# Routing by tile beside w_out, expert 0's rows from one-hot products, and the first norm interleaved with the first chunks

## The chip, the cores and the metric

The kernel runs on one core of a Trainium2 chip. The metric is the device time of one execution in microseconds (us). One execution was also recorded by the hardware profiler; its rows are what is quoted below. PE is TensorE, DVE VectorE, ACT ScalarE, POOL GpSimd, SP SyncE.

## The reference, cut to what matters

Input x is 512 tokens by 1024 features, all in float32.

```python
h = layer_norm(x, ln_in_g, ln_in_b)
proj = h @ w_in            # 1024 x 9240: q, k, v, gates of two mixers
y_gla = gla_branch(...) @ w_gla_proj      # gated linear attention, 4 heads, chunks of 64
y_fox = fox_branch(...) @ w_fox_proj      # causal attention with forgetting, 8 heads
mixed = sigmoid(z_gla) * y_gla + sigmoid(z_fox) * y_fox
h = layer_norm(ALPHA * h + mixed @ w_out, ln_mix_g, ln_mix_b)
logits = h @ w_router + b_router          # 32 experts
top_val, top_idx = top_k(logits, 4); gates = softmax(top_val)
# every token goes to its 4 experts: ((clip(up) + 1) * glu(gate)) @ w_down[e] + b_down[e]
h = layer_norm(ALPHA * h + sum_of_gated_experts, ln_ffn_g, ln_ffn_b)
```

## The kernel before

Each engine has its own hand-written instruction list; semaphores tie them together, and the lists set the order. The 512 tokens are four tiles (TT = 4) of 128 partitions.

**Products.** A product with weights is done in three passes (`passes`, L1282 to L1284): each operand is split into a high part (ACT copies it to float32r, `whi`, `hT_hi`, `xT_hi`) and a low part (DVE subtracts, `wlo`, `hT_lo`, `xT_lo`), and PE multiplies high by high, high by low and low by high. SP loads weights by 1 MB tiles into a ring (`raw`, 4 slots, later 6), ACT and DVE split them, PE uses them. The projections, w_gla_proj, w_fox_proj and w_out are 44 such chunks of 256 columns (`DENSE`).

**Start.** SP loads the four tiles of x, then chunks. ACT issues two broadcast loads of the norm's gain and offset to 128 partitions, takes the first square root (`std(0)`), then issues ten small loads (small weights, biases, the router's weights), then goes on with square roots and high parts. DVE takes statistics of a tile (`norm_stats`), norms it (`norm_apply`, L896 to L898), and makes low parts (`h_lo` L910, `dense_lo` L903). PE turns the normed tile (`turn_h`, transposes, L1289), and does chunk 0 as four units of one token tile each, and then chunk 1. A `hook(s)` after each half chunk s puts other work in between: the small product (s = 1), the gate path, later the two mixers.

**w_out and routing.** w_out is done by token tile, four groups j of 256 columns. DVE adds the product to h (L1057), norms the tile and PE turns it (`turn_h2`); the logits are a product with h2T stationary and the router weights `w_rt` moving (L1487), 16 float32 products of 32 columns for two tiles at a time. DVE then does top-4 (`max`, `max_index`), a one-hot table, membership, gates and `vals` for all four tiles at once. PE makes each token's position within its expert (L1495), DVE compares it with iota (`slots`, L1122), and `table(x, e)` (L1504) multiplies slots and vals, so that 128 slots get a token number and a gate for expert e. POOL gathers the tokens' rows from `h2_dram` (`gather`, L546, indirect DMA), PE turns them (`turn_x`) and ACT and DVE split them to `xT_hi` and `xT_lo`. An overflow list (more than 128 tokens for one expert) is built in between (L1509 to L1513) and ends in `routed`.

**Experts.** For expert i: eight tiles of `gate_up`, bias (L1533), turn of the next expert's rows, then four tiles of `down` for expert i - 1, bias (L1552), then `turn_a` of the activations `act_t`. DVE: `swiglu_in` (L1162, L1164), `swiglu_out` (L1170), the low parts of weight tiles (`tile_lo`, L1068; ACT's `tile_hi` is L808). For expert 0 there is no down; `turn_a(0, 1)` stands ahead of expert 1's first gate-up tile. POOL scatters results into `acc_dram` with an adding DMA, for which h2 was first copied there (L535, L536).

## Time and profile before

| | |
|---|---|
| median of 3 runs | 1903.54 us (1903.32 to 1905.56) |
| the profiled execution's own time | 1902.3 us |
| its span, first to last instruction | 1900.7 us |
| PE busy | 1806.0 us, 95% |
| DVE busy | 1383.6 us, 73% |
| ACT busy | 1081.5 us, 57% |
| moved by DMA | 495.55 MB, mean 261 GB/s |

A group row of the page has line, engine, operation, output and inputs with their shapes, the count, then busy us and mean ns of one. In a row of a timeline, what stands in square brackets is the idle time of that engine ahead of it and what ended it. A PE record is one weight load with one pass of a product; a product of plain float32 operands is two records.

### The profile page before, as it was taken

To read this page: it belongs to the slowest core of one execution; us is meant where nothing else is said; L and a number is where in the kernel's file an instruction comes from. 1 tells how busy PE (TensorE), PEld (TensorE's weight loads), DVE (VectorE), ACT (ScalarE), POOL (GpSimd) and SP (SyncE) were. 2 spreads that over 40 slices of the span, in tenths; PEclk is the share of its full clock that TensorE was granted. 3 is DMA by queue.
4 is the path that set the end of the run, shared out by engine and by line. 5 is a ranking of instruction groups with operands and counts; after the bars stand their busy time and mean duration, and the time that the engine had idled before them with its cause. 6 is when DMAs were issued, how large, how long until landed. Compare 5 with 4: busy or idle time off the path is not lost.

```text
span 1900.7 us, 25902 instructions
## 1 busy us (share of the span) xinstructions
PE 1806.0 (95%) x9120; PEld 1493.2 (79%) x9121; DVE 1383.6 (73%) x1368; ACT 1081.5 (57%) x858; POOL 303.4 (16%) x260
## 2 busy tenths in 40 slices
PE   4999999999999967999999999999999999999993
PEld 4897797778888856888888888888888888888882
DVE  5224522433435467999999999999999999999996
ACT  2433323455322035777777777777677777777771
POOL 2000000000000011221221221222222222222111
PEclk9999999999999868999999999999999999999997
DMA  8332122212232367999999999999999999999983
GB/s 249 114 89 67 45 82 74 58 54 68 89 110 89 133 251 263 358 361 375 382 358 370 381 365 361 388 367 361 381 371 359 386 373 356 382 376 360 374 330 117
DMA packets 140706, 495.55 MB, mean 261 GB/s; under 512 B 18212, under 2 KB 63652, under 8 KB 107890
## 3 DMA queue, kind: packets, MB, share of 16 engines
q1 hardware_dynamic: 119168, 455.11, 63.3%
q0 software_dynamic: 17200, 38.03, 7.6%
q10 hardware_dynamic: 4290, 1.73, 0.4%
q8 instruction: 35, 0.57, 0.1%
q14 instruction: 13, 0.11, 0.0%
HBM read 477.52 MB, written 26.48 MB: 265 GB/s over the span
## 4 chain that ended last, share of the span: by engine, by line
PE 92%; DVE 4%; DMA 1%; ACT 1%; issue 1%; ACTq 0%; POOL 0%; DVEq 0%; POOLq 0%
PE psA L1282 21%; PE psA L1284 20%; PE psA L1283 20%; PE psX L1283 6%; PE psX L1284 6%; PE psX L1282 6%; PE psX L1289 4%; PE psX L1435 1%; PE psX L1421 1%; PE psX L1394 1%; PE psA L1533 1%; PE psA L1487 1%; DVE wlo L1068 1%; PE psX L1552 1%; PE psX L1504 1%
## 5 line engine op out<-in xcount | busy, mean ns | idle before, releaser
L1068 DVE TENSOR_TENSOR wlo<-raw,whi 128x2048 fp32r<-128x2048 f32 x384 | 859.6, 2285 | 33.8 <-ACT whi L808 33.8
L808 ACT CAST whi<-raw 128x2048 fp32r<-128x2048 f32 x384 | 727.7, 1911 | 229.3 <-PE psA L1284 217.7
L1282 PE MATMUL psA<-whi,xT_hi 128*128 128x512 f32 x1024 | 406.7, 397 | 2.4 <-issue 2.4
L1284 PE MATMUL psA<-whi,xT_lo 128*128 128x512 f32 x1024 | 400.2, 391 | 0.0
L1283 PE MATMUL psA<-wlo,xT_hi 128*128 128x512 f32 x1024 | 400.1, 391 | 0.0
L1284 PEld LDWEIGHTS psA<-whi,xT_lo 128*128 128x128 f32 x1024 | 192.9, 188 | 41.6
L1282 PEld LDWEIGHTS psA<-whi,xT_hi 128*128 128x128 f32 x1024 | 193.3, 189 | 41.0 <-issue 2.8
L1283 PEld LDWEIGHTS psA<-wlo,xT_hi 128*128 128x128 f32 x1024 | 193.3, 189 | 38.1
L1282 PE MATMUL psX<-whi,aT_hi 128*128 128x512 f32 x512 | 203.0, 397 | 5.9 <-DVE aT_lo L1158 5.9
L1283 PE MATMUL psX<-wlo,aT_hi 128*128 128x512 f32 x512 | 200.5, 392 | 0.0
L1284 PE MATMUL psX<-whi,aT_lo 128*128 128x512 f32 x512 | 200.3, 391 | 0.0
L903 DVE TENSOR_TENSOR wlo<-raw,whi 128x2048 fp32r<-128x2048 f32 x40 | 91.6, 2290 | 138.3 <-ACT whi L627 138.2
L557 POOL DMA_INDIRECT acc_dram<-y_t,didx x31 | 113.9, 3674 | 358.6 <-ACT y_t L839 347.4
L1282 PE MATMUL psA<-hT_hi,whi 128*128 128x512 f32 x416 | 165.5, 398 | 0.0
L1284 PE MATMUL psA<-hT_hi,wlo 128*128 128x512 f32 x416 | 162.2, 390 | 0.0
L1283 PE MATMUL psA<-hT_lo,whi 128*128 128x512 f32 x352 | 137.3, 390 | 0.0
L562 POOL DMA_DIRECT2D bgu<-bgu_dram x64 | 35.2, 550 | 511.4 <-PE psA L1533 511.0
L1282 PEld LDWEIGHTS psX<-whi,aT_hi 128*128 128x128 f32 x512 | 96.8, 189 | 25.4 <-issue 6.1
L1284 PEld LDWEIGHTS psX<-whi,aT_lo 128*128 128x128 f32 x512 | 96.7, 189 | 20.4
L1283 PEld LDWEIGHTS psX<-wlo,aT_hi 128*128 128x128 f32 x512 | 96.8, 189 | 19.3
L627 ACT CAST whi<-raw 128x2048 fp32r<-128x2048 f32 x40 | 76.3, 1908 | 40.6 <-PE psA L1284 40.6
L546 POOL DMA_INDIRECT xg<-h_dram,gidx x33 | 90.0, 2728 | 44.6 <-DVE gidx L1140 32.4
(297 smaller groups left out, 2383.3 us busy)
## 6 DMA issues: line engine op xcount, KB each, us to landing
raw<-in_w_gate_up SPq DMA_DIRECT2D x256, 1024.0 KB, 8.3
raw<-in_w_down SPq DMA_DIRECT2D x128, 1024.0 KB, 8.3
raw<-in_w_in SPq DMA_DIRECT2D x32, 1024.0 KB, 5.5
raw<-in_w_gla_proj SPq DMA_DIRECT2D x4, 1024.0 KB, 5.1
raw<-in_w_fox_proj SPq DMA_DIRECT2D x4, 1024.0 KB, 5.2
raw<-in_w_out SPq DMA_DIRECT2D x4, 1024.0 KB, 5.1
acc_dram<-h POOLq DMA_DIRECT2D x5, 512.0 KB, 5.1
xt<-in_x SPq DMA_DIRECT2D x4, 512.0 KB, 8.3
```

The lines of the kernel that those rows point to most:

```text
L546: g.indirect_dma_start(xg[:], None, h2_dram, bass.IndirectOffsetOnAxis(ap=gidx[:, 0:1], axis=0), bounds_check=token_bound, oob_is_err=Fals ...
L557: g.indirect_dma_start(acc_dram, bass.IndirectOffsetOnAxis(ap=didx[:, 0:1], axis=0), y_t[:], None, bounds_check=row_bound, oob_is_err=True ...
L562: g.dma_start(bgu[part:P:32, :], bgu_rows[part, e, :].rearrange("(n c) -> n c", c=512)).then_inc(bgu_in, 16)
L627: s_.copy(whi[:, c % SPL, :], raw[:, c % RAW, :]).then_inc(hi_ready, 1)
L808: s_.copy(xsplit(c)[0], xraw(slot)).then_inc(hi_ready, 1)
L903: v.tensor_tensor(wlo[:, c % SPL, :], raw[:, c % RAW, :], whi[:, c % SPL, :].bitcast(F32), ALU.subtract).then_inc(lo_ready, 1)
L1068: v.tensor_tensor(lo, xraw(slot), hi.bitcast(F32), ALU.subtract).then_inc(lo_ready, 1)
L1282: mm(dst, sh, mh, start=first, stop=False)
L1283: mm(dst, sh, ml, start=False, stop=False)
L1284: return mm(dst, sl, mh, start=False, stop=last)
L1289: ins = nc.tensor.transpose(dst[:, k // 4, (k % 4) * P:(k % 4 + 1) * P], src[:, k * P:(k + 1) * P], ident[:])
L1394: ins = mm(psX[:, half, tok], state[:, n, half * P:(half + 1) * P], gq[:, h, tok], start=True, stop=True)
```

## The change

The first norm's gain and offset are loaded as rows of 512 and spread over the partitions by four products with a row of ones. SP issues the ten small loads, behind the first four chunks. The first two chunks are done unit by unit, with the norms and low parts between; the hooks 1 to 8 move to 3 to 10. In w_out, each token tile is normed in halves, turned, routed (now `w_rt` stationary, h2T moving) and its top-4 chosen while later tiles are multiplied. Expert 0's transposed rows are made by `pick`: h2's tiles as stationary operand and the one-hot slots of expert 0 as moving operand, summed over the tiles in psA, with no gather. Its token table follows during its gate-up tiles, the overflow list during those of expert 1. The copies to acc_dram follow the gather for expert 1. `turn_a(0, 1)` stands behind expert 1's third gate-up tile. The core of the diff:

```diff
+            if c == 0:
+                load_x(2)
+                load_x(3)
+            if c == RAW - 1:
+                load_params()
...
-        gather(1, None)
         load_bgu(0)
         load_bdn(0)
+        gather(2, None)
+        for t in range(TT):
+            g.dma_start(acc_tiles[t], h2[:, t, :]).then_inc(acc_out, 16)
+        g.dma_start(acc_tiles[TT], h2[:, 0, :]).then_inc(acc_out, 16)
+        pool.wait_ge(gu_done, 1)
+        load_bgu(1)
+        gather(3, 2)
...
-        gather(2, 1)
-        pool.wait_ge(gu_done, 1)
-        load_bgu(1)
-        gather(3, 2)
...
-        act.dma_start(lnin_g[:], bcast(a["ln_in_g"])).then_inc(lnin_in, 16)
-        act.dma_start(lnin_b[:], bcast(a["ln_in_b"])).then_inc(lnin_in, 16)
+        act.dma_start(ln_rows[0:33:32, :], a["ln_in_g"].rearrange("(n c) -> n c", c=512)).then_inc(lnin_in, 16)
+        act.dma_start(ln_rows[64:97:32, :], a["ln_in_b"].rearrange("(n c) -> n c", c=512)).then_inc(lnin_in, 16)
...
+        s_.activation(warm, eps_c, ACT.Sqrt)
+        act.wait_ge(lnin_spread, 1)
+        s_.copy(lnin_g[:], psA[:, 0:2, :].rearrange("p b c -> p (b c)")).then_inc(lnin_ready, 1)
+        s_.copy(lnin_b[:], psA[:, 2:4, :].rearrange("p b c -> p (b c)")).then_inc(lnin_ready, 1)
         std(0)
-        w_in = a["w_in"][0].rearrange("(k p) c -> p k c", p=P)
-        act.dma_start(sm_raw[:, :, 0:RANK], w_in[:, :, C_LOW:C_LOW + RANK]).then_inc(small_in, 16)
-        act.dma_start(sm_raw[:, :, RANK:RANK + FH], w_in[:, :, C_FF:C_FF + FH]).then_inc(small_in, 16)
-        act.wait_ge(w_up_zero, 1)
-        act.dma_start(w_up[0:RANK, :], a["w_gla_gate_up"][0]).then_inc(params_in, 16)
-        act.dma_start(w_up[32:33, :], a["b_gla_gate"]).then_inc(params_in, 16)
-        act.dma_start(b_f, bcast(a["b_forget"][0], FH)).then_inc(params_in, 16)
-        with nc.allow_non_contiguous_dma(reason="256 gains onto partitions"):
...
+            h2_turned_out(t)
+            std(TT + t + 1)
+            logits_out(t)
+            if t < TT - 2:
+                gate_exp(t)
+        h2_turned_out(TT - 1)
+        tile_hi(0, 1, 0, 0)
+        gate_exp(TT - 2)
+        logits_out(TT - 1)
+        tile_hi(1, 1, 1, 1)
+        gate_exp(TT - 1)
+        tile_hi(2, 1, 2, 2)
 
...
+        x_stats(0)
+        x_stats(1)
+        dve.wait_ge(lnin_ready, 2)
+        x_apply(0)
+        dense_lo(0)
+        x_stats(2)
+        h_lo(0)
+        x_apply(1)
         dense_lo(1)
+        x_stats(3)
+        h_lo(1)
+        x_apply(2)
+        h_lo(2)
+        x_apply(3)
+        h_lo(3)
         dve.wait_ge(small_hi, 1)
         v.tensor_tensor(sm_lo[:], sm_raw[:], sm_hi[:].bitcast(F32), ALU.subtract).then_inc(small_lo, 1)
...
+        def mix_norm(t):
+            for half in range(2):
+                cols = slice(512 * half, 512 * (half + 1))
+                dve.wait_ge(wo_done, 2 * t + half + 1)
+                v.scalar_tensor_tensor(h2[:, t, cols], h2[:, t, cols], ALPHA, psA[:, 2 * (t % 2) + half, :], ALU.mult,
                                        ALU.add).then_inc(wo_evac, 1)
-                dve.wait_ge(wo_evac, t + 1)
-                norm_stats(t, h2[:, t, :], seq)
-            if t >= 1:
-                norm_apply(TT + t - 1, t - 1, h2[:, t - 1, :], lnmix_g[:], lnmix_b[:], seq).then_inc(h2_norm, 1)
+                dve.wait_ge(wo_evac, 2 * t + half + 1)
+                seq.mark(v.bn_stats(stats[:, t, 6 * half:6 * half + 6], h2[:, t, cols]))
+            seq.join()
+            v.bn_aggr(mv[:, t, :], stats[:, t, :]).then_inc(var_ready, 1)
+            dve.wait_ge(std_ready, TT + t + 1)
+            seq.link(v.reciprocal(rstd[:, t:t + 1], rstd[:, t:t + 1]))
+            for half in range(2):
+                cols = slice(512 * half, 512 * (half + 1))
+                row = h2[:, t, cols]
+                seq.link(v.scalar_tensor_tensor(row, row, mv[:, t, 0:1], lnmix_g[:, cols], ALU.subtract, ALU.mult))
+                v.scalar_tensor_tensor(row, row, rstd[:, t:t + 1], lnmix_b[:, cols], ALU.mult,
+                                       ALU.add).then_inc(h2_norm, 1)
+
...
+        def choose(t):
+            dve.wait_ge(lg_turned, t + 1)
+            seq.link(v.tensor_tensor(logits[:, t, :], psX[:, 1, t * E:(t + 1) * E], b_rt[:], ALU.add))
+            seq.link(v.max(top_v[:, t, :], logits[:, t, :]))
+            seq.link(v.max_index(top_i[:, t, :], top_v[:, t, :], logits[:, t, :]))
+            seq.link(v.tensor_copy(top_f[:, t, :], top_i[:, t, :]))
+            seq.link(v.tensor_tensor(hot[:], iota[:, 0:E].unsqueeze(2).broadcast_to(shape),
+                                     top_f[:, t, 0:TOPK].unsqueeze(1).broadcast_to(shape), ALU.is_equal))
+            v.tensor_reduce(member[:, t, :], hot[:], AX_X, ALU.add).then_inc(mem_ready, 1)
+            dve.wait_ge(mem_ready, t + 1)
+            seq.mark(v.tensor_scalar(posb[:, t, :], member[:, t, :], BIG, -BIG, ALU.mult, ALU.add))
+            v.tensor_scalar(logits[:, t, :], logits[:, t, :], top_v[:, t, 0:1], None, ALU.subtract).then_inc(ge_in, 1)
+
...
+        def place(t):
+            seq.join()
+            dve.wait_ge(pos_done, max(t + 1, 2))
+            seq.link(v.tensor_tensor(posm[:, t, 0:E], posb[:, t, :], psX[:, 1, P + t * E:P + (t + 1) * E], ALU.add))
+            v.tensor_scalar(slots[:, t, :], iota[:, 0:P], posm[:, t, 0:1], None, ALU.is_equal).then_inc(placed, 1)
...
+        mix_norm(0)
+        mix_norm(1)
+        choose(0)
+        seq.mark(weigh(0))
+        mix_norm(2)
+        choose(1)
+        seq.mark(weigh(1))
+        dve.wait_ge(wo_done, 2 * TT - 1)
+        place(0)
+        place(1)
+        mix_norm(3)
+        choose(2)
+        place(2)
+        tile_lo(0, 0, 0)
+        choose(3)
+        place(3)
+        seq.mark(weigh(2))
+        dve.wait_ge(xT_hi_s, 1)
+        v.tensor_tensor(xT_lo[:], psA[:, 0:2, :].rearrange("p b (k c) -> p (b k) c", k=4), xT_hi[:].bitcast(F32),
+                        ALU.subtract).then_inc(xT_lo_s, 1)
+        tile_lo(1, 1, 1)
+        seq.mark(weigh(3))
         seq.join()
-        for t in range(TT):
-            seq.mark(v.max(top_v[:, t, :], logits[:, t, :]))
...
         swiglu_in(0)
         turned_lo(xT_hi_s, 2, xT_hi, xT_lo, xT_lo_s)
+        step_lo(1, 1)
         swiglu_out(0)
-        turned_lo(aT_hi_s, 1, aT_hi, aT_lo, aT_lo_s)
+        step_lo(1, 2)
+        step_lo(1, 3)
         seq.join()
         start = seq.used
...
+            if first:
+                turned_lo(aT_hi_s, 1, aT_hi, aT_lo, aT_lo_s)
+            for c in range(XSPL + 1, XSPL + 5):
...
+        for b in range(4):
+            row = slice(32 * b, 32 * b + 1)
+            ins = mm(psA[:, b, :], ones[row, :], ln_rows[row, :], start=True, stop=True)
+        ins.then_inc(lnin_spread, 1)
...
+        first_unit(0, 0)
+        turn_h(1)
+        first_unit(1, 0)
+        first_unit(0, 1)
+        turn_h(2)
+        first_unit(1, 1)
+        first_unit(0, 2)
+        turn_h(3)
+        first_unit(1, 2)
+        first_unit(0, 3)
+        first_unit(1, 3)
...
+        def route(t):
+            if t >= 1:
+                pe.wait_ge(lg_out, t)
+            for k in range(KT):
+                if k % 4 == 0:
+                    pe.wait_ge(h2T_evac, 2 * t + k // 4 + 1)
+                ins = mm(psX[0:E, 0, 0:P], w_rt[:, k, :], h2T[:, k, t * P:(t + 1) * P], start=k == 0, stop=k == KT - 1)
+            ins.then_inc(lg_done, 1)
+
...
+        def pick(t):
+            pe.wait_ge(placed, t + 1)
+            if t == 0:
+                pe.wait_ge(wo_evac, 2 * (TT - 1))
+                pe.wait_ge(blank_ready, 1)
+                for b in range(2):
+                    mm(psA[:, b, :], blank[:], iota[0:1, :], start=True, stop=False)
+            for k in range(KT):
+                ins = mm(psA[:, k // 4, (k % 4) * P:(k % 4 + 1) * P], h2[:, t, k * P:(k + 1) * P],
+                         slots[:, t, :].bitcast(F32), start=False, stop=t == TT - 1 and k % 4 == 3)
+            if t == TT - 1:
+                ins.then_inc(xt_done, 1)
 
         pe.wait_ge(dve_half, 2 * (NCD - NPROJ))
...
+                if j == 0 and t >= 2:
+                    turn_logits(t - 2)
+                if j == 2 and t >= 1:
+                    turn_h2(t - 1, 0)
+                    turn_h2(t - 1, 1)
+                if j == 2 and t == TT - 1:
+                    positions(0)
+                    positions(1)
+            if t >= 1:
+                route(t - 1)
+        pick(0)
+        turn_h2(TT - 1, 0)
+        turn_logits(TT - 2)
+        turn_h2(TT - 1, 1)
+        route(TT - 1)
+        positions(2)
+        turn_logits(TT - 1)
+        pick(1)
+        pick(2)
+        positions(3)
+        pick(3)
 
         def table(x, e):
...
+            if c == 1:
+                table(0, 0)
+            if c == 3:
+                pe.wait_ge(tab_ready, 1)
                 table(1, 1)
...
-        turn_a(0, 1)
...
+                if first:
+                    if c == 2:
+                        turn_a(0, 1)
+                    if c == 4:
+                        overflow_counts()
+                    if c == 5:
+                        overflow_ranks()
                 if c == GUC - 2:
+                    if first:
+                        overflow_list()
```

How the first instructions stand on ACT, which gives the first norm its square roots (DMA rows are issues; small holds the roots). Before:

```order
L638 ACTIVATE small<-small 128x1
L647 DMA sm_raw<-in_w_in 128x8x16
L648 DMA sm_raw<-in_w_in 128x8x8
L650 DMA w_up<-in_w_gla_gate_up 16x512
L651 DMA w_up<-in_b_gla_gate 1x512
L652 DMA small<-in_b_forget 128x8
L654 DMA small<-in_g_gla_norm 128x2x1
L655 DMA w_rt<-in_w_router 128x8x32
L656 DMA b_rt<-in_b_router 128x32
L657 DMA bias_raw<-in_b_gate_up 128x512
L658 DMA bias_raw<-in_b_down 128x256
L638 ACTIVATE small<-small 128x1
```

After:

```order
L658 DMA ln_rows<-in_ln_in_g 2x512
L659 DMA ln_rows<-in_ln_in_b 2x512
L683 ACT_TABLE_LOAD
L683 ACTIVATE small<-small 128x1
L685 COPY lnin_g<-psA 128x1024
L686 COPY lnin_b<-psA 128x1024
L676 ACTIVATE small<-small 128x1 x2
L665 CAST whi<-raw 128x2048
L670 CAST hT_hi<-psX 128x8x128
L676 ACTIVATE small<-small 128x1
L665 CAST whi<-raw 128x2048
L670 CAST hT_hi<-psX 128x8x128
```

The ten small loads are gone from between the first and the second root; two copies of the spread rows stand ahead of the roots.

DVE at the start, where normed tiles (xt, L897 and L898 before, L957 and L958 after) and the low parts of tiles and chunks are made. Before:

```order
L896 RECIPROCAL small<-small 128x1
L897 SCALAR_TENSOR_TENSOR xt<-xt,small,lnin_g 128x1024
L898 SCALAR_TENSOR_TENSOR xt<-xt,small,lnin_b 128x1024
L889 BN_STATS small<-xt 128x6
L890 BN_STATS small<-xt 128x6
L891 BN_AGGR small<-small 128x2
L896 RECIPROCAL small<-small 128x1
L897 SCALAR_TENSOR_TENSOR xt<-xt,small,lnin_g 128x1024
L898 SCALAR_TENSOR_TENSOR xt<-xt,small,lnin_b 128x1024
L910 TENSOR_TENSOR hT_lo<-psX,hT_hi 128x8x128
L903 TENSOR_TENSOR wlo<-raw,whi 128x2048
```

After:

```order
L956 RECIPROCAL small<-small 128x1
L957 SCALAR_TENSOR_TENSOR xt<-xt,small,lnin_g 128x1024
L958 SCALAR_TENSOR_TENSOR xt<-xt,small,lnin_b 128x1024
L963 TENSOR_TENSOR wlo<-raw,whi 128x2048
L949 BN_STATS small<-xt 128x6
L950 BN_STATS small<-xt 128x6
L951 BN_AGGR small<-small 128x2
L970 TENSOR_TENSOR hT_lo<-psX,hT_hi 128x8x128
L956 RECIPROCAL small<-small 128x1
L957 SCALAR_TENSOR_TENSOR xt<-xt,small,lnin_g 128x1024
L958 SCALAR_TENSOR_TENSOR xt<-xt,small,lnin_b 128x1024
L963 TENSOR_TENSOR wlo<-raw,whi 128x2048
```

Chunk 0's low part moved ahead of the first tile's low part, and the second norm behind both.

PE from w_out's last product to expert 0's first gate-up product (h is the normed rows, member the membership). Before:

```order
L1495 MATMUL psA<-member_104,strict 128x32
L1495 MATMUL psA<-member_104,ones 128x32 x2
L1495 MATMUL psA<-member_104,strict 128x32
L1495 MATMUL psA<-member_104,ones 128x32 x3
L1495 MATMUL psA<-member_104,strict 128x32
L1497 MATMUL psA<-ones,member_104 96x1 x4
L1504 MATMUL psX<-vals,slots 128x4 x4
L1509 MATMUL psA<-ovflag,strict 96x1
L1511 MATMUL psA<-ovhot,small 1x16
L1512 MATMUL psA<-ovhot,small 1x16
L1513 MATMUL psA<-ones,ovflag 1x1
L1289 MATMUL psX<-ident,xg 128x128 x8
```

After:

```order
L1601 MATMUL psX<-h2T,w_rt 32x128 x8
L1627 MATMUL psA<-iota,blank 128x512 x2
L1629 MATMUL psA<-slots,h_89 128x128 x8
L1592 MATMUL psX<-ident,h_89 128x128 x4
L1610 MATMUL psX<-ident,logitsT 128x32
L1592 MATMUL psX<-ident,h_89 128x128 x4
L1601 MATMUL psX<-h2T,w_rt 32x128 x8
L1618 MATMUL psX<-member,ones 128x32 x2
L1618 MATMUL psX<-member,strict 128x32
L1610 MATMUL psX<-ident,logitsT 128x32
L1629 MATMUL psA<-slots,h_89 128x128 x16
L1618 MATMUL psX<-member,ones 128x32 x3
```

The turn of gathered rows (xg), the table and the overflow products are gone from here; four groups of eight products of slots and h have come (the last, for tile 3, stands two rows further).

## Rows read from the trace of the kernel before

**Rows 1.** The page: the span, the engines' busy time, and one of its costliest groups.
```profile
span 1900.7 us, 25902 instructions
...
PE 1806.0 (95%) x9120; PEld 1493.2 (79%) x9121; DVE 1383.6 (73%) x1368; ACT 1081.5 (57%) x858; POOL 303.4 (16%) x260
...
L808 ACT CAST whi<-raw 128x2048 fp32r<-128x2048 f32 x384 | 727.7, 1911 | 229.3 <-PE psA L1284 217.7
```

**Rows 2.** Waits of PE in 0 to 60 us: us in total, times, longest.
```profile
PE psX L1289 <- DVE xt L898: 13.6, 1, 13.6
PE psX L1289 <- DVE wlo L903: 12.0, 1, 12.0
```

**Rows 3.** Timeline of 0 to 62 us: start, length, engine, line, operation.
```profile
6.40 0.69 DVE L889 BATCH_NORM_STATS2 small<-xt 128x6 f32<-128x512 f32 x1 [6.28 <-DMA xt<-in_x]
...
12.15 1.28 DVE L898 SCALAR_TENSOR_TENSOR xt<-xt,small,lnin_b 128x1024 f32<-128x1024 f32 x1
...
15.38 4.47 ACTq L656 DMA_DIRECT2D b_rt<-in_b_router  x1
...
20.97 0.29 ACT L638 ACTIVATE small<-small 128x1 f32<-128x1 f32 x1 [11.37 <-issue]
...
25.15 2.28 DVE L903 TENSOR_TENSOR wlo<-raw,whi 128x2048 fp32r<-128x2048 f32 x1
```

**Rows 4.** Windows: stretch, length, busy time of each engine, granted clock, DMA.
```profile
27.50:62.60 35.10, 35.06 (x248) 31.80 (x248) 18.46 (x18) 12.22 (x17) 3.17 (x6) 1.00 0.60 187
601.10:649.40 48.30, 48.08 (x400) 47.84 (x400) 15.64 (x21) 3.85 (x7) 4.25 (x8) 1.00 0.25 89
649.40:696.40 47.00, 26.52 (x128) 25.62 (x128) 25.67 (x72) 12.86 (x11) 8.17 (x14) 0.52 0.78 291
696.40:722.70 26.30, 26.26 (x109) 21.31 (x110) 17.42 (x29) 13.78 (x8) 3.15 (x1) 0.89 0.61 233
722.70:758.90 36.20, 26.53 (x122) 21.75 (x123) 27.87 (x26) 19.77 (x13) 4.15 (x3) 0.86 0.71 268
758.90:795.20 36.30, 36.30 (x174) 29.52 (x173) 34.09 (x29) 26.70 (x17) 9.13 (x6) 1.00 0.94 335
```

**Rows 5.** Waits of PE in 600 to 760 us.
```profile
PE psX L1289 <- DVE act_t L1170: 9.7, 1, 9.7
PE psA L1495 <- DVE member L1105: 6.2, 1, 6.2
```

**Rows 6.** Timeline of 599 to 775 us: VectorE, then ScalarE, then GpSimd.
```profile
648.36 1.22 DVE L1057 SCALAR_TENSOR_TENSOR h<-h,psA 128x1024 f32<-128x1024 f32 x1 [6.93 <-PE psA L1284]
...
673.82 0.18 DVE L1092 RECIPROCAL gate_r<-gate_s 128x4 f32<-128x4 f32 x1
...
683.93 0.87 DVE L1122 TENSOR_SCALAR slots<-iota,posm 128x128 fp32r<-128x128 f32 x4
...
665.33 1.28 ACT L823 ACT_TABLE_LOAD   x1
...
694.07 1.01 ACT L830 CAST xT_hi<-psX 128x1024 fp32r<-128x1024 f32 x1 [13.37 <-PE psX L1289]
...
664.49 2.10 POOL L535 DMA_DIRECT2D acc_dram<-h  x4 [7.13 <-DMA h_dram<-h]
```

**Rows 7.** The chain that ended last, its longest pieces: start, length, what.
```profile
62.70 3.63 PE psX L1361 x8
...
266.52 4.04 PE psX L1413 x40
...
635.94 0.87 PE psX L1289 x8
...
653.87 1.97 PE psX L1289 x8
655.84 6.67 PE psA L1487 x32
...
687.42 4.61 DMA xg<-h_dram,gidx
```

More of the change, by code:

```diff
@@ L840, in y_evac @@
                           scale=queue[:, 0, 1:2]).then_inc(y_ready, 1)
-        turned_hi(xt_done, 1, xT_hi, xT_hi_s)
+        act.wait_ge(xt_done, 1)
+        s_.copy(xT_hi[:], psA[:, 0:2, :].rearrange("p b (k c) -> p (b k) c", k=4)).then_inc(xT_hi_s, 1)
+        tile_hi(3, 1, 3, 3)
         for c in range(XSPL, GUC):
@@ L849, in _ @@
         silu(0)
+        for c in range(XSPL, XSPL + 3):
+            step_hi(1, c)
         turned_hi(aturn_done, 1, aT_hi, aT_hi_s)
-        with act.Fori(1, E) as i:
+        for c in range(XSPL + 3, STEPC):
+            step_hi(1, c)
+        turned_hi(xt_done, 3, xT_hi, xT_hi_s)
+        silu(1)
+        for c in range(XSPL):
+            step_hi(2, c)
+        y_evac(0, 4)
+        turned_hi(aturn_done, 2, aT_hi, aT_hi_s)
+        with act.Fori(2, E) as i:
             for c in range(XSPL, STEPC):
@@ L1134, in take_table @@
             dve.wait_ge(tab_done, x + 1)
-            if not (isinstance(x, int) and x == 0):
-                dve.wait_ge(xg_in, 16 * x)
+            if not (isinstance(x, int) and x <= 1):
+                dve.wait_ge(xg_in, 16 * (x - 1))
             chain.mark(v.tensor_reduce(queue[:, 3, 1:2], psD[:, 0, 2:4], AX_X, ALU.add))
@@ L1172, in _ @@
         tile_lo(2, 2, 2)
-        turned_lo(xT_hi_s, 1, xT_hi, xT_lo, xT_lo_s)
-        tile_lo(3, 3, 3)
+        take_table(0, seq)
+        for b in range(3):
+            ins = v.tensor_copy(member3[:, :, b * E:(b + 1) * E], member[:])
+        ins.then_inc(counts_in, 1)
         slot_rows(slice(1, 2), iota[:, 0:P])
+        for c in range(3, 5):
+            tile_lo(c % XRAW, c, c)
         shift_queue(seq)
@@ L1579, in _ @@
         turn_x(1)
-        turn_a(0, 1)
         def body(i):
+            first = isinstance(i, int) and i == 1
             split_ready(xT_hi_s, xT_lo_s, i + 1)
@@ L1595, in body @@
             pe.wait_ge(tab_ready, i + 3)
+            if first:
+                pe.wait_ge(routed, 1)
             for q in range(DNC):
```

398 lines of the change are left out of this document (205 added, 193 removed).

## The prediction

> **What bounds the kernel now.** I read the page first: TensorE (PE) is busy for 1806.0 of 1900.7 us, a share of 95% [rows 1]. From the third expert on, PE has no gap: expert pass 1's second half and pass 2 fill 36.3 us with 36.3 us of work (the last of [rows 4]). So a gain can only come from PE's idle time and from its time at the low clock, in two places. The profiled execution took 1902.3 us; its span is 1900.7 us, and the median of the runs is 1903.5 us, 1.2 us above it.
>
> The start: the waits show PE standing 13.6 us for the first normed tile and 12.0 us for the split of chunk 0 [rows 2]. The timeline says why: VectorE (DVE) has its first statistics at 6.4 us and tile 0 is normed at 13.4, but tile 1's square root comes at 21.0, because ScalarE (ACT) issues ten small loads between its first and second root, one of them standing 4.47 us [rows 3]. DVE, behind that, ends chunk 0's low half at 27.4 [rows 3]. From 27.5 to 62.6 PE then works without a gap [rows 4].
>
> The routing: the projection w_out ends at 649.1; between 649.4 and 696.4 PE works only 26.5 of 47.0 us, at a mean granted clock of 0.52 of 2.4 GHz [rows 4]. It waits 6.2 us for the membership, then for the gather of 4.61 [rows 7], and later 9.7 for act_t between the first two gate-up passes [rows 5]. The gate-up pass of expert 0 takes 26.3 us and the stretch to the end of the next one 36.2, with 9.7 idle in it [rows 4].
>
> **The change, part by part.**
>
> *Spread of the norm's gain and offset.* Two 512 KB broadcast loads go; four products of one row by 512 columns and two ACT copies come. No row has a small load so early: I bound its landing between 3 and 7 us and take 4.5 (x tile 0, much larger, is there at 6.4 [rows 3]). Four 512-column f32 products took 3.63 us at the full clock [rows 7]; at the low one everything takes about twice as long (eight transposes 1.97 against 0.87 [rows 7]), so 7 us, to 11.5. Two copies of 128x1024 at 1.0 (as xT_hi's [rows 6]) give 13.5, root and reciprocal 13.9. So tile 0 is normed at 16.6, three us *later* than before. This cover is no free one: the spread is now what the first norm waits for.
>
> *Order on DVE and the moved loads.* Behind it stand chunk 0's low half (2.28), the statistics of tile 2 (1.5) and tile 0's low half (1.2): 18.9, 20.4, 21.6. ACT has no loads in between, so its roots are never late. The first projection product starts at 21.7, and from there PE has three turns, eight units, the small product: the same work that before followed without a gap from 27.5. I checked the cover: PE's first unit is at the low clock (5.1 us), to 26.8, while DVE norms tile 1 by 24.3 and splits chunk 1 by 26.5; tile 1's low half is there at 30, when PE still has chunk 1's first unit; later tiles keep 0.5 to 1.5 us ahead. **Gain 5.8 us** (ends: 2, with the load at 7 us and a bubble per tile; 8, with it at 3). The hooks of the gate path move two half-chunks later; PE stays full there, so nothing.
>
> *w_out, turns and logits by tile.* The four tiles take 46.1 us of products and 0.95 per turn (48.3 with two turns [rows 4]). Three turns, two route groups, two small transposes and three position products now stand inside. With w_rt stationary a product streams 128 columns of f32: the nearest row is 40 such records in 4.04 us, 0.10 each [rows 7], two per product, eight products, 1.7 us a tile (ends: 0.9, if a record did it as in a transpose; 3.4 as now, 32 records in 6.67 at the low clock [rows 7]). w_out ends at 654.6, 5.5 later than before.
>
> *The routing chain.* DVE's last norm is in halves: a sum of half of 1.22 [rows 6] with a little for its start, 0.7, then 0.8 for statistics, 0.7 for root and reciprocal, and for each half two operations of half of 1.28, 1.4: rows ready at 658.5 and 659.9. PE meanwhile does the last-but-one route (656.4) and the blank and pick products of tile 0: 1.8 + 1.7, to 659.8. Turn, two half copies, route: 663.0, positions 663.6. ACT stands between: split of weight tile 0 (1.9 [rows 1]), exponent with its table load (1.28 [rows 6] and 0.2), logits copy: 665.5. Choosing is eight linked small operations at 0.2 (a reciprocal of 4 elements took 0.18 [rows 6]): 1.6 us, behind a low split that ends at 666.7, so 668.3. PE: picks 1 and 2 to 669.2, positions 670.1, slot row 670.8 (0.22 each, four took 0.87 [rows 6]), pick 3 to 672.7, ACT 673.9, DVE 675.2. **First gate-up product at 675.3 instead of 696.4: 21.1 us.** The gather (4.61 [rows 7]), the wait for DRAM before it and the overflow list are off this path; ends for the pick: 0.9 and 3.4 us a tile.
>
> *Expert 0 and 1.* A gate-up tile takes 2.73 on PE (36.3 less some 3.5 of turns, table and biases, over 12). But DVE sets this pass: from 675.2 it has seven splits (16.0), the last weights (1.7), two tables with their queue shifts (2.2), membership copies (0.5), two groups of slot rows (1.7) and half a us of waiting, to 697.8. PE so starts tile 5 at 693.5, and three tiles, a table and the bias end at 702.7, against 722.7: 20.0 left. Then gate and up are taken (2.3), the next rows split, PE waits some 2.8 (703.7 to 706.5), and act_t's turn stands after the third tile instead of ahead of the first: the second bias ends at 732.0 against 758.9. **26.9 us kept**; the 9.7 wait is mostly gone, and the overflow products (1.6) now stand there. POOL copies 2.5 MB to acc_dram at 690 instead of 664 [rows 6], among weight loads; at the 335 GB/s of the busy stretch [rows 4] that is 7.5 us of all queues; the tiles have about that slack, so 0, and 7 as the end. Behind 732 DVE is some 0.6 us later against PE than before, which the steady passes (34.1 busy of 36.3 [rows 4]) give back.
>
> *The clock.* So far PE was at full speed. Before, it stopped at 649.1 and the mean to 696.4 was 0.52 [rows 4]; the products on w_rt, 6.67 us without a gap, did not bring it back [rows 7]. After, PE has gaps of 2.0 (663.6), 2.6 (672.7) and 2.8 us (703.7). Any may lower it; all routing products behind the first at the low clock cost 7, gate-up tiles up to 3 each time, in part hidden behind DVE. I take 4.5 (ends 0 and 13). [...]
>
> Sum: 5.8 + 26.9 - 4.5 = 28.2 us off 1902.3: 1874.1, and 1.2 more for the median: 1875.
>
> **The rivals.**
> A, as summed, 1867 to 1881: 62%.
> B, the low clock stays from w_out into expert 0 and falls again after it: 13 instead of 4.5, 1884. For it, the same stage ran at 0.52; against it, PE has 9 us more work there without a gap. 15%.
> C, the start gives nothing (the spread is later than I think, or each tile leaves a bubble): 1881. 8%.
> D, the copies to acc_dram make weight tiles 10 to 13 late: 7 more, 1882. 5%.
> E, no clock fall and a start of 8: 1867 less what is shorter than I took, 1865 or below. 5%.
> F, routing chain twice as slow on DVE's links, so that the 28 us go (0.2%, about 4 us, is what a measurement of this kernel can tell from no change): 3%.
> G, slower. The ten small loads now stand in SP's queue ahead of chunk 4's weights. One stood 4.47 us at issue [rows 3]. Chunk 4 is needed at about 62, and its load can go out at about 20; each us beyond 62 is a us. It would have to arrive after 90 to end slower than before. 2%. [...]
>
> **How the numbers follow.** The time is A's. B, C and D end by 1887, so 1865 to 1887 leaves out half of E, the worst of B and D, F and G, and pairs of them: about 2 in 10. Faster by over 0.2%: all but F and G, 0.95; within 0.2%: 0.03; slower: 0.02.
>
> **What would show it.** The waits of PE in the first 60 us: the long one ends near 16.6, the next near 21.7, and none over 1.5 after it. The gate path's 512-column products start near 57 instead of 62.7. The first gate-up product stands 74 us behind w_out's first (95.3 before), near 669.5 in the new span. The second bias ends near 726. Windows between w_out's end and it give the clock. I am wrong if PE's wait for act_t stays, if the choosing takes over 3 us a tile, or if DVE, not PE, sets the pace beyond the second expert.

## The result, and the profile after

The changed kernel takes 1880.77 us (median of 4 runs, 1877.45 to 1882.37), beside 1903.43 for the kernel before in the same session: a ratio of 0.9878, 95% interval 0.9864 to 0.9891. That is 22.7 us less. The forecast was 1875, its range 1865 to 1887.

The profiled execution of the changed kernel is the slowest of its four: 1882.37 us, span 1880.7. The rows of its page that answer to [rows 1]:

```profile
span 1880.7 us, 26088 instructions
...
PE 1811.5 (96%) x9192; PEld 1492.8 (79%) x9193; DVE 1391.0 (74%) x1412; ACT 1090.5 (58%) x876; POOL 302.2 (16%) x259
...
PEclk9999999999999988999999999999999999999997
```

PE is busy 5.5 us longer and the span is 20.0 us shorter, so 25.5 us of its idle time are gone. In the clock's line (40 slices, tenths) two eights stand at slices 15 and 16, from 658 to 752 us. PE's waits from 0 to 60 us, which answer to [rows 2]:

```profile
PE psA L1400 <- DMA ln_rows<-in_ln_in_b: 7.2, 1, 7.2
PE psX L1392 <- DVE xt L958: 5.2, 1, 5.2
PE psA L1385 <- DVE hT_lo L970: 2.7, 1, 2.7
```

Three waits end at 7.2, 14.6 and 19.3 us, and none follows. PE's waits from 655 to 760 us, which answer to [rows 5]:

```profile
PE psA L1385 <- DVE xT_lo L1238: 4.3, 1, 4.3
PE psX L1392 <- DMA xg<-h_dram,gidx: 3.6, 1, 3.6
PE psA L1385 <- issue: 2.4, 1, 2.4
PE psA L1385 <- DVE wlo L1181: 2.1, 2, 1.2
PE psX L1610 <- ACT logitsT L854: 1.5, 1, 1.5
PE psA L1629 <- DVE slots L1175: 0.7, 1, 0.7
```

The wait of 9.7 for act_t and that of 6.2 for the membership are gone. New are 3.6 for the rows (xg) of expert 1 and 4.3 for their low part. The windows of this stretch, which answer to [rows 4] (length, busy time of PE, weight loads, DVE, ACT, POOL, granted clock, DMA):

```profile
655.00:672.00 17.00, 12.46 (x90) 11.41 (x87) 9.14 (x32) 10.86 (x11) 2.58 (x5) 0.89 0.90 362
672.00:700.00 28.00, 25.89 (x112) 20.30 (x112) 20.50 (x40) 14.10 (x9) 10.18 (x6) 0.95 0.71 247
700.00:710.00 10.00, 2.06 (x13) 1.68 (x9) 6.28 (x9) 4.92 (x4) 2.22 (x3) 0.61 1.00 376
710.00:738.00 28.00, 28.00 (x129) 22.37 (x130) 24.21 (x27) 14.64 (x9) 1.11 (x2) 0.89 0.81 307
```

Between 700 and 710 PE works 2.06 of 10 us, and the mean granted clock is 0.61 (in these records it is always one of two levels, 1.2 or 2.4 GHz, so a mean says how long each was granted); in the stretch behind it PE has no gap, but a mean clock of 0.89. Why PE stands there is read off the timeline of DVE and POOL:

```profile
687.39 0.15 DVE L1233 TENSOR_SCALAR gidx<-psX 128x1 uint32<-128x1 f32 x1
687.45 0.87 DVE L1215 TENSOR_SCALAR slots<-iota,posm 128x128 fp32r<-128x128 f32 x4
688.23 6.69 DVE L1181 TENSOR_TENSOR wlo<-raw,whi 128x2048 fp32r<-128x2048 f32 x3
...
703.69 0.16 DVE L1230 TENSOR_REDUCE small<-psX 128x1 f32<-128x2 f32 x1 [8.27 <-DMA xg<-h_dram,gidx]
```
```profile
688.44 7.48 POOL L582 DMA_INDIRECT xg<-h_dram,gidx  x1 [22.16 <-DVE gidx L1233]
695.92 2.18 POOL L609 DMA_DIRECT2D acc_dram<-h  x4
```

DVE writes the row numbers (gidx) at 687.5, and 0.2 us before POOL begins to issue the gather DVE begins three low splits without a gap. The issue (POOL's handing over of the DMA) lasts 7.48 us and ends at 695.92, 1.0 us behind the end of the third split (694.92). In the kernel before, the first gather was issued in 1.10 us and its rows were there after 4.61 [rows 7]; here they come 15.1 us after the issue begins. The answer on the tile xg for 679 to 697 us has one line on it:

```profile
DMA to landing us min/median/max: 15.1/15.1/15.1
```

DVE then stands 8.27 us for the rows, because take_table(2) overwrites the row numbers and must wait for the gather, and everything behind it in DVE's list is late: the split of expert 1's first tile, gate and up, xT_lo.

The table measures the stages from w_out's first product (us), as the timelines give them. The predicted column is the prediction's own times, brought to the starts of the biases. The last three columns belong to the experiments below.

| | before | predicted | after | e5 | e10 | e12 |
|---|---|---|---|---|---|---|
| w_out's first product, from the span's start | 601.1 | 595.3 | 594.8 | 594.9 | 595.4 | 592.9 |
| expert 0's first gate-up product | 95.3 | 74.2 | 77.1 | 77.1 | 75.5 | 77.1 |
| expert 0's bias | 121.0 | 101.0 | 104.7 | 106.3 | 101.7 | 103.7 |
| expert 1's first gate-up product | 133.9 | 105.4 | 115.1 | 110.7 | 111.8 | 108.3 |
| expert 1's bias | 157.1 | 130.2 | 142.7 | 136.9 | 136.6 | 133.1 |

### The profile page after: what moved, and what is told of

Same layout as the page of the kernel before. It is cut to its first block, busy times and chain, and to the rows that moved or that the text cites. A ratio compares the mean times of both kernels' runs of the same rounds, so it can differ in the third digit from the quotient of the medians.

```text
span 1880.7 us, 26088 instructions
## 1 busy us (share of the span) xinstructions
PE 1811.5 (96%) x9192; PEld 1492.8 (79%) x9193; DVE 1391.0 (74%) x1412; ACT 1090.5 (58%) x876; POOL 302.2 (16%) x259
## 4 chain that ended last, share of the span: by engine, by line
PE 93%; DVE 3%; DMA 2%; ACT 1%; issue 1%; ACTq 0%; POOL 0%; SPq 0%; DVEq 0%; POOLq 0%
PE psA L1385 21%; PE psA L1386 21%; PE psA L1387 21%; PE psX L1386 6%; PE psX L1387 6%; PE psX L1385 6%; PE psX L1392 4%; PE psX L1555 1%; PE psX L1541 1%; DMA xg<-h_dram,gidx 1%; PE psX L1514 1%; PE psA L1717 1%; PE psX L1736 1%; PE psX L1680 1%; PE psX L1556 1%
## 5 line engine op out<-in xcount | busy, mean ns | idle before, releaser
L1386 PEld LDWEIGHTS psX<-wlo,aT_hi 128*128 128x128 f32 x512 | 96.8, 189 | 19.3
L1385 PE MATMUL psA<-whi,hT_hi 128*128 128x256 f32 x320 | 95.5, 298 | 2.7 <-DVE hT_lo L970 2.7
```

Of the source, the lines that this page charges most:

```text
L1385: mm(dst, sh, mh, start=first, stop=False)
L1386: mm(dst, sh, ml, start=False, stop=False)
```

## The experiments

Each run's ratio is to the kernel before on the same chip. An interval is some 0.15% (3 us) to either side, so two variants less than about 4 us apart are not told apart by time, and the trace has to speak. A trace is one execution, though, and how often its clock falls is in part that execution's luck, as e1 shows first.

### The two halves alone (e1, e11)

e1 is the kernel before with only the start of the change; e11 has only the rest.

> The kernel before with only the start of the change: rows of gain and offset spread by four products, small loads in SP's queue, the first two chunks unit by unit, the hooks moved to 3 to 10. Routing and experts as before. Theory 1 (the two halves of the change add up, the start is worth the 6.3 us by which w_out's first product stood earlier in the profiled execution of the changed kernel): 1897, ratio 0.9967, 1895 to 1899. Theory 2 (the start is worth the 9.9 us by which the first projection product came earlier, and the changed kernel's extra stretches at the low clock in the mixers were that execution's alone): 1893.5, ratio 0.9948. Theory 3 (the start gives nothing of its own): 1903. The windows of the granted clock between 90 and 230 us tell theory 1 from 2.

> The kernel before with only the second half of the change: routing by tile beside w_out, expert 0's rows from one-hot products, the new order of experts 0 and 1; the start as before. With the start alone at a ratio of 0.9965 (6.7 us), the two halves add up to the changed kernel if this one stands at 0.991 (1886 to 1888). A ratio of 0.988 or below would mean that the start's gain is given back when both are in.

e1: 1896.53 us, ratio 0.9965 (0.9951 to 0.9978). e11: 1889.20, ratio 0.9926 (0.9911 to 0.9942), with runs from 1883.9 at a mean clock of 0.988 to 1894.4 at 0.981. So the start is worth 6.7 us and the rest 14 by its ratio (15.2 between the medians); theory 1 of e1 holds. The product of the ratios is 0.989, beside 0.9878 for both: they add up within the intervals, and no loss from having both is seen. e11's own expectation (0.991) was just missed. The clock in the mixers, windows of 60 to 250 us, of the kernel before and then of e1:

```profile
60.00:250.00 190.00, 184.24 (x1169) 160.32 (x1168) 68.50 (x70) 67.27 (x80) 0.00 (x0) 0.98 0.23 67
```
```profile
60.00:250.00 190.00, 184.24 (x1144) 160.18 (x1143) 72.25 (x74) 64.82 (x77) 0.00 (x0) 0.96 0.22 65
```

PE's work is the same to 0.01 us, but the mean clock is 0.98 in one and 0.96 in the other. e7 and e9 below have the same program up to here, and show 0.98 and 0.96, with w_out's first product at 589.7 and 595.0: how often the clock falls in the mixers differs from one execution to the next, and is worth up to 5 us. Whether the new start also makes it likelier is open. Of the twelve traces with it, eleven spend 13.7 to 17.1 us between 60 us and w_out at the low clock and only e7 6.8, while the two traces with the old start (the kernel before and e11) have 6.8; but over whole executions the mean clock of e1's five (0.972 to 0.974) lies inside that of the kernel before (0.971 to 0.976).

### Is the gather held up by DVE, or by crowded queues? (e2, e3, e5)

Theory L: the issue of the gather can't end while a low split runs. Theory Q: its rows are late because weight tiles and the copies to acc_dram fill the queues. e2 makes DVE wait for the issue, e3 puts the copies ahead of the gather, and e5 gives DVE small work in between:

```diff
         gather(2, None)
+        pool.sem_inc(issued, 1)
...
         slot_rows(slice(2, 3), iota[:, 0:P])
+        dve.wait_ge(issued, 1)
```

That is e2; e5 changes DVE's list alone:

```diff
         slot_rows(slice(2, 3), iota[:, 0:P])
+        for _ in range(6):
+            seq.link(v.tensor_copy(gate_s[:], gate_s[:]))
         for c in range(5, GUC):
             tile_lo(c % XRAW, c, c)
```

> The changed kernel, but VectorE waits, after the slot rows for expert 2, until GpSimd has issued the gather for expert 1, and only then starts its run of three low splits (6.7 us). Theory L (the issue of the gather, 7.48 us in the profiled execution, stands because VectorE's low splits run without a gap; it ended 1.0 us behind the end of their run): the issue takes 1.1 us, the rows land near 697 instead of 703.6, the 8.3 us in which VectorE stood for them are gone but for 1 to 2, the splits start 1.3 us later, and expert 1's first gate-up product comes some 5 us earlier, with the stretch at the low clock behind it shorter or gone: 4 to 10 us less than the changed kernel, 1871 to 1877, ratio 0.983 to 0.986. Theory Q (the DMA queues are crowded by weight tiles, whatever VectorE does): the issue still takes over 4 us, the landing stays near 15 us behind, and the wait costs 1.3 us: 1880 to 1883.

> The changed kernel, but the five copies of h2 to acc_dram (2.5 MB) stand ahead of the gather for expert 1 in GpSimd's queue, as before, so that they are issued near 666 instead of 696. Theory Q2 (the copies, issued right behind the gather among weight tiles, are what makes its rows land late): the rows land 4 to 8 us earlier: 1872 to 1877. Theory L: the issue of the gather still takes 7 us or so, since VectorE's run of low splits is the same; VectorE still stands over 6 us for the rows: 1878 to 1883, no difference from the changed kernel beyond what a measurement can tell.

> The changed kernel with six small linked copies of four elements a row (0.2 us each) on VectorE behind the slot rows for expert 2, so that GpSimd's issue of the gather for expert 1, which begins 1.05 us behind the table, finds no low split running. In the run with VectorE waiting for the issue, that wait held nothing up (the run of splits began at the same 0.2 us ahead of the issue's record), yet the issue took 3.1 us and ended 1.0 behind the first split, not 7.5 behind the third. Theory L (the issue ends 1.0 us behind the end of a low split, and of how many is chance): with the pause it takes 1.1 us, rows land 7 to 8 us behind its end, VectorE stands under 1 us for them: 5 to 8 us less than the changed kernel, 1872 to 1876, ratio 0.9835 to 0.9855. Theory Q (crowded queues): the issue may be short, but the rows still land over 12 us behind its start; 1880 and above.

| | us | ratio | issue | rows there after |
|---|---|---|---|---|
| the changed kernel | 1880.77 | 0.9878 | 7.48 | 15.1 |
| e2 | 1875.89 | 0.9852 (0.9837 to 0.9867) | 3.08 | 9.3 |
| e3 | 1878.98 | 0.9866 (0.9851 to 0.9882) | 7.45 | 13.3 |
| e5 | 1877.86 | 0.9864 (0.9847 to 0.9882) | 1.11 | 4.8 |

e5's timeline of DVE, then of POOL, and the line on xg's landing:

```profile
686.00 0.87 DVE L1215 TENSOR_SCALAR slots<-iota,posm 128x128 fp32r<-128x128 f32 x4
686.78 1.50 DVE L1264 COPY gate_s<-gate_s 128x4 f32<-128x4 f32 x6
688.32 6.69 DVE L1181 TENSOR_TENSOR wlo<-raw,whi 128x2048 fp32r<-128x2048 f32 x3
...
698.51 0.16 DVE L1230 TENSOR_REDUCE small<-psX 128x1 f32<-128x2 f32 x1 [3.01 <-PE psX L1682]
```
```profile
686.99 1.11 POOL L582 DMA_INDIRECT xg<-h_dram,gidx  x1 [20.66 <-DVE gidx L1233]
688.11 2.17 POOL L609 DMA_DIRECT2D acc_dram<-h  x4
```
```profile
DMA to landing us min/median/max: 4.8/4.8/4.8
```

With 1.5 us of small copies ahead of the same three splits the issue takes 1.11 us and the rows are there after 4.8 us instead of 15.1, among the same weight tiles and with the copies to acc_dram right behind. DVE no longer waits for them, only for PE's table. That settles it for theory L, and against Q as the cause. e3 agrees: the issue still takes 7.45 us with the copies out of the way, and the rows come 1.8 us sooner, which is what the copies add in these two executions. Its time is 1.8 us below the changed kernel's, inside the intervals.

Not every DMA that POOL issues is held up. In e5 the four copies to acc_dram, plain DMAs, are issued while the first split runs, in 2.17 us; in the changed kernel, with no split running, in 2.18. What the splits hold up is the indirect DMA, which reads its row numbers from a tile.

e5's saving between the biases (the table: 115.1 to 110.7 for expert 1's first product) is partly paid for: its first bias is 1.6 us later, since DVE sets the pace of expert 0's pass and now has 1.5 us more to do. In time it is 2.9 us below the changed kernel, which the intervals don't tell from it; 5 to 8 were expected.

e2 went otherwise than its edit meant. DVE's run of splits began as before 0.2 us ahead of the issue's record (689.43 and 689.63), so the semaphore had been raised before the issue's record begins. Yet the issue ended 1.0 us behind the *first* split, and took 3.08 us, not the 1.1 expected. From the third expert on, the issues take 2.8 us (gather) and 3.7 (adding DMA), and end 1.0 and 1.5 us behind a split's end. Where a split ends during an issue, no trace here has the issue ending less than 0.9 us behind it. Why the issue sometimes gets in behind the first split and sometimes behind the last of a run stays open.

The Trainium skill ("SBUF — State Buffer", SBUF: two separate sides) says that GpSimd shares a pair of SBUF ports with VectorE as an exclusive lock, and that a VectorE operation with two SBUF inputs holds it only against a GpSimd operation that reads SBUF. The low split has two such inputs, raw and whi. The Trainium skill reports there that such an operation did not stall a DMA. For the plain copies the trace agrees (2.17 and 2.18 us); for the gather it doesn't (7.48 against 1.11), and the measurement decides. That its reading of the row numbers is what waits would fit both, but no run separates it. That a hold can last through three operations the page doesn't say.

### The turn of act_t put back (e4)

`turn_a(0, 1)` stands ahead of expert 1's first gate-up tile again.

> The changed kernel, but the turn of expert 0's activations stands ahead of expert 1's first gate-up tile again, with its two splits where they were before. In the changed kernel xT_lo was there at 709.8 and act_t at 713.1, so PE would stand at least 3.3 us more, and then the splits of act_t (2.3 us) compete with those of the weight tiles. If the move of the turn carries what the prediction gave it: 4 to 9 us slower than the changed kernel, 1885 to 1889. If the late rows of expert 1 have eaten what the move gives: within 2 us of it, 1879 to 1883.

1885.11 us, ratio 0.9907 (0.9894 to 0.9921), 4.3 us slower than the changed kernel, the low end of what was expected. The medians carry this: the profiled execution of e4 is its fastest (1881.50), and has expert 1's bias 143.1 behind w_out's first product, only 0.4 later than the changed kernel's, with less time at the low clock on the way. The wait has come back, in e4's waits of PE from 655 to 760:

```profile
PE psX L1389 <- DVE act_t L1248: 7.9, 1, 7.9
PE psX L1389 <- DMA xg<-h_dram,gidx: 3.1, 1, 3.1
```

### Tables earlier, the first norm from PSUM, and the spread undone (e6, e7, e8)

In e6 PE's tables move as follows, DVE takes them accordingly, with four small copies as a pause ahead of tile 4:

```diff
-            if c == 1:
+            if c == 0:
                 table(0, 0)
-            if c == 3:
+            if c == 1:
                 pe.wait_ge(tab_ready, 1)
                 table(1, 1)
```

In e7 PE spreads the rows to psX first and then to psA, ScalarE takes both roots and chunk 0's high part ahead of its copies, and DVE norms tile 0 from psX:

```diff
-        dve.wait_ge(lnin_ready, 2)
-        x_apply(0)
+        dve.wait_ge(lnin_spread, 1)
+        norm_apply(0, 0, xt[:, 0, :], psX[:, 0:2, :].rearrange("p b c -> p (b c)"),
+                   psX[:, 2:4, :].rearrange("p b c -> p (b c)"), seq).then_inc(h_norm, 1)
```

> The changed kernel with the tables of experts 0 and 1 one or two gate-up tiles earlier on PE (behind the first and the second), VectorE taking each without the 1.6 and 0.9 us it stood for them, the copies for the overflow counts behind the slot rows for expert 2, and four small linked copies as a pause before the low splits of tiles 4 to 7. The gather for expert 1 is then issued near 683.5 instead of 688.4. Expected from the rows of the changed kernel: rows of expert 1 there at 692, no wait of VectorE or PE for them, first bias 2 to 3 us earlier (VectorE sets this pass), expert 1's first gate-up product near 700.5 instead of 709.9: 9 us, and with the stretch at the low clock behind it gone up to 12: 1868 to 1873, ratio 0.982 to 0.984. If the loss is in crowded queues, the wait for the rows only moves: 1877 to 1881.

> The changed kernel, but the four spread products are done twice, first to psX, from where VectorE norms tile 0 itself, then to psA for the two copies; ScalarE takes both roots and the high split of chunk 0 before the copies. If the start is a chain of load, products, copies, norm, turn, with PE full behind it, tile 0 is normed 1.5 to 2.4 us earlier (it began at 11.82; the products end at 9.3) and the kernel is faster by that: 1878.5 to 1879.5 where the changed kernel has 1880.8, ratio 0.9865. If the tiles behind tile 0 set the pace: no difference.

> The changed kernel with the gain and offset loaded by two broadcasts of 512 KB again, no spread products and no copies. My prediction gave the spread a first norm 3.2 us later than with the loads (16.6 against 13.4); in the trace of the changed kernel tile 0 is normed at 14.4. If the loads beside x cost nothing, tile 0 would be normed by 13.4 and the kernel be 1 us faster. If they hold up x's tiles and chunk 0 (before, tile 1 of x was there at 9.2, now at 6.1, and tile 0 at 6.4, now at 4.65), it is 1 to 3 us slower: 1882 to 1884, ratio 0.989.

e6: 1876.32, ratio 0.9858 (0.9840 to 0.9877); the issue takes 1.27 us, the rows are there 4.9 us after its start, and expert 1's bias stands 136.0 behind w_out's first product instead of 142.7. In time e6 is 4.5 us below the changed kernel, not the 8 to 12 expected: PE still waits 3.3 us for xT_lo (gate, up and this split stand behind each other on DVE), and 6.8 us at the low clock follow. e7: 1877.69, 0.9863 (0.9846 to 0.9881); the first projection product is at 16.96 instead of 19.25, 2.3 us earlier, as expected, and the rest of the 3.1 us between the medians is inside the interval. e8: 1880.66, 0.9880 (0.9862 to 0.9899), no difference. With the broadcast loads tile 0 is normed a us earlier, but its statistics begin at 6.25 instead of 4.65 and chunk 0 comes later; in e8's timeline of ACT:

```profile
12.30 1.90 ACT L665 CAST whi<-raw 128x2048 fp32r<-128x2048 f32 x1 [1.30 <-DMA raw<-in_w_in]
```

The projections begin at 19.15, as with the spread. So the spread is worth nothing either way; the start's gain lies in the order of units and in the small loads off ACT, which no run takes apart.

### The clock (e10), and the repairs together (e9, e12)

e10 is the changed kernel with products that nobody reads in PE's gaps; e9 is e6 and e7 together; e12 is e9 with filler in the gaps left to it.

```diff
+        for _ in range(2):
+            mm(psX[:, 1, :], ident[:], iota[:], start=True, stop=True)
         split_ready(xT_hi_s, xT_lo_s, 1)
...
         gate_up_bias(0)
+        for _ in range(3):
+            mm(psX[:, 1, :], ident[:], iota[:], start=True, stop=True)
         turn_x(1)
+        for _ in range(4):
+            mm(psX[:, 1, :], ident[:], iota[:], start=True, stop=True)
```

> The changed kernel with products that nobody reads (ident by iota, 512 columns, 0.9 us each at the full clock) in PE's gaps: two ahead of expert 0's first gate-up product, three ahead of the turn of expert 1's rows, four behind it. The waits themselves stay. Theory K (PE's waits in this stretch are what puts the clock down; after them 3.4, 6.8 to 13.7 us were at 1.2 GHz in each profile): no low stretch, or under 4 us, between 655 and 740, and expert 1's pass (27.5 us from its first product to its bias) takes 24 to 25; 3 to 5 us faster than the changed kernel: 1876 to 1878, ratio 0.986. Theory M (the low stretches come from elsewhere, or filler doesn't count as work): the granted clock is as before and the kernel is the same or up to 2 us slower: 1880 to 1883.

> The changed kernel with both repairs: the tables of experts 0 and 1 earlier with the pause on VectorE, and tile 0 normed from PSUM. If they add: 2.3 us (the projections began at 16.96 instead of 19.25) and 5 to 7 us (second bias 136.0 us behind w_out's start instead of 142.7) less than the changed kernel's 1880.8: 1872 to 1874, ratio 0.983 to 0.9845, below every run so far. If one hides the other or the clock takes it back: 1875 to 1877.

> Both repairs together with filler products in what is left of PE's gaps: two ahead of expert 0's first gate-up product (a wait of 2.4 us), three behind the turn of expert 1's rows (a wait of 3.4 us). Theory K: no low stretch between 600 and 740, where the run with both repairs had 3.4 and 6.8 us; in time half of these 10.2 us at most, 3 to 5 us less than it: 1868.5 to 1870.5, ratio 0.981 to 0.9825. If the filler holds up what it stands ahead of, or the clock falls elsewhere: 1873 to 1875, no gain.

e10: 1876.79, ratio 0.9862 (0.9846 to 0.9879). The window of 655 to 740 us, of the changed kernel and then of e10:

```profile
655.00:740.00 85.00, 70.41 (x350) 57.57 (x348) 62.13 (x107) 46.52 (x32) 17.39 (x19) 0.88 0.82 307
```
```profile
655.00:740.00 85.00, 77.85 (x398) 60.28 (x397) 67.65 (x112) 48.67 (x34) 21.95 (x19) 1.00 0.89 333
```

The gather is as late as ever (issue 7.47, rows after 14.8), and the clock never falls. Expert 1's pass takes 24.9 us instead of 27.6, and its bias stands 136.6 behind w_out's first product instead of 142.7. For the gap ahead of expert 1's pass theory K holds: all ten traces with the new routing and no filler have a low stretch that begins between 697 and 706, of 3.4 to 13.7 us, and the two with filler there, e10 and e12, have none.

How much of the 6.1 us is the filler's is another matter. e8 and e11 have no filler, but their clock too stayed up as far as expert 0's bias, and they stand at 137.8; e10's filler is worth 1.2 us to them, and 1.6 in expert 1's pass (24.9 against 26.5). The other 4.9 is what the changed kernel's profiled execution lost beside theirs. In time e10 is 4.0 us below the changed kernel by the medians and 3 by the ratios, at the edge of what is told apart. Nor do waits explain every low stretch: in e2, e4, e5, e7 and e9 one of 3.4 us begins during the first pick, some 6 us ahead of PE's first wait of the routing (in e5 at 654.1, the wait at 660.5).

e9: 1873.40, ratio 0.9837 (0.9823 to 0.9850), 7.4 us below the changed kernel where e6 and e7 alone are 4.5 and 3.1: the repairs add. e12: 1871.16, ratio 0.9821 (0.9807 to 0.9834), faster than both kernels; its median is 9.6 us below the changed kernel's. Its granted clock, window of 655 to 745:

```profile
655.00:745.00 90.00, 84.37 (x421) 67.06 (x420) 77.81 (x114) 57.77 (x38) 16.91 (x21) 0.98 0.91 349
```

PE works 84.4 of 90 us here, fillers included. 3.4 us at the low clock remain before expert 0's first tile. e12's expectation for the ratio is met, its us are 0.7 above the range, and it is 2.2 us below e9 where 3 to 5 were expected: by time the filler's part isn't told from nothing.

## Why the prediction was right, and where it missed

The direction, the mechanisms and the range were right; the gain was 22.7 us instead of 28. In the two profiled executions the account is 6.3 us up to w_out's first product (5.8 forecast), 14.4 from there to expert 1's bias (26.9 less 4.5 for the clock, 22.4), and 0.7 lost behind it: 20.0 of span, and the other executions of the changed kernel, at 0.984 to 0.986 of the clock instead of 0.983, are 1 to 5 us quicker.

*The start.* The size is right by errors that cancel, which is luck. The small load landed at 7.1 us, just past the late end of the bound (4.5 taken). The four products took 2.1 us, not 7; the chain of the changed kernel has them:

```profile
2.12 4.99 DMA ln_rows<-in_ln_in_b
7.24 2.12 PE psA L1400 x8
...
11.82 1.30 DVE xt L957
13.14 1.28 DVE xt L958
```

So tile 0 was normed at 14.4 instead of 16.6, and the projections began at 19.25 instead of 21.7. From there PE ran without a wait, as forecast. That is 8.3 us ahead of the 27.5 of [rows 4]; by w_out 6.3 are left, and the changed kernel's mixers ran at a mean clock of 0.96 in this execution, as e1's, beside 0.98 before. Without that the start would have brought more than the 5.8 forecast. One sign was stated wrongly: the gate path moved behind chunk 2, so its products stand at 65.0, not 57.

*w_out and routing.* Expert 0's first product stood at 77.1 instead of 74.2 behind w_out's first. 1.6 of this is the low clock: e8, e10 and e11, whose clock did not fall there, have 75.5. The parts were near: 1.9 us for a route (1.7 forecast), 2.05 for a pick (1.7 to 1.9), 1.8 for the choosing (1.6), so rival F is out.

*Expert 0's pass.* 27.5 us to the start of its bias, 26.8 forecast; where the clock stayed up (e8, e10, e11) it was 26.1 to 26.2. DVE counts in it as forecast: 1.5 us more on DVE made it 29.3 in e5.

*The step that failed* is "Then gate and up are taken (2.3), the next rows split, PE waits some 2.8 (703.7 to 706.5)". It gave expert 1's gather no time, since I had put the gathers down as off the path. That holds for expert 0's, which is gone. But with 19 us less from w_out to expert 1's first product, the gather of expert 1 has no slack left, and it now stands in DVE's run of low splits. Expert 1's first product came 10.4 us after expert 0's bias instead of 4.4. e5 shows it: with the issue free it comes 4.3 us after (4.6 in e2, 4.9 in e6). The 4.61 of [rows 7] was the wrong row to judge by: during the 1.10 us of that gather's issue DVE had only small operations, and its next low split began 0.15 us ahead of the issue's end, while in the changed kernel the gather stands where a run of splits begins. The kernel before could have told. Its rows on the tile xg give the 33 gathers' issue (ns) and the time from an issue's start to landing, and only the first is of the short kind:

```profile
L546 POOL DMA_INDIRECT xg<-h_dram,gidx x33: 1100/2773/3152, 687.4 to 1808.2; - x33
...
DMA to landing us min/median/max: 4.6/10.3/10.6
```

*The clock* was sized 4.5 (0 to 13). Between two executions, the changed kernel's and e10's, it measures 6.1; against e8 and e11, whose clock fell only behind expert 0's bias, 1.2. It is a term of each execution, so that the size came near is in part luck. It overlaps with the failed step, since the longest low stretch (13.7 us from 702.3) stands in the long wait: e5 alone gives 5.8 of the 12.5 us missing at expert 1's bias, e10 alone 6.1, and e12 9.6.

*act_t's turn* is worth 4.3 us by the medians (e4). *Rival D* (the copies make weight tiles late) didn't happen: PE's waits for wlo are 2.1 us with the copies there and with them early. The copies cost 1.8 us of the gather's landing instead. *Rival C* is refuted by e1, *rival B* by the windows, where the clock was at 0.95 in expert 0's pass. *Rival G*: no wait for chunk 4.

## What to carry to other kernels

A step moved off the critical path keeps its price only if its new neighbours leave it alone: look at what each engine it touches does at the new place, VectorE for an indirect DMA that GpSimd issues. Take its price not from its shortest instance in the trace, but from one with the neighbours that it will get. When its issue lasts longer than that shortest, try a short pause of small operations in front of VectorE's run; here 1.5 us of them brought it from 7.48 to 1.11. And where PE must wait a few us ahead of a dense stretch, products that nobody reads can keep the clock up; here they saved 1.6 to 2.7 us of the pass behind the wait, which only the trace shows with any certainty. What a low stretch costs is to be compared over several traces, not two.

## What the runs showed of the hardware

- The issue of an indirect gather on GpSimd takes 1.1 to 1.3 us where no low split on VectorE ends during it, 2.8 (the median, in every trace) among the single splits of the steady passes, and 7.45 to 7.48 beside three in a row. Four plain DMAs from the same queue take 2.17 us beside splits and 2.18 without.
- The rows of a kernel's first gather land 3.1 to 4.1 us behind the end of an issue that was not held up (before, e1, e5, e6, e9, e12), and 5.9 to 7.6 behind one that was (e2, e3, e4, e7, e8, e10, e11 and the changed kernel).
- Four products of one row by 512 columns, on partitions 0, 32, 64 and 96, took 2.1 us while eight transposes took 1.94, as at the low clock [rows 7]. Two such products on the same row took 2.0 us at the full clock (the blank products of the changed kernel). That the four ran beside each other fits; it wasn't tried.
- The same program spends between 6.8 and 17 us of the mixers at the low clock from one execution to the next (e7 and e9), and w_out's first product stands at 589.7 or 595.0 for it. Whole executions follow: the kernel before ran in 1900.8 us at a mean clock of 0.976 and in 1907.8 at 0.971.
